# Own copies of the weight units around the joint normalisations, and an order of work that follows expected durations

## The chip, the cores and the metric

The kernel is one program on one core of a Trainium2 chip. The metric is device time in microseconds (us), lower is better. The engines are TensorE (PE), VectorE (DVE), ScalarE (ACT), GpSimd (POOL) and SyncE (SP), which issues the large loads. Each runs its own instructions in the order in which the program gives them to it, and they meet only at semaphores.

## The reference

Two transformer blocks of two layers each, in float32, on 256 tokens of width 1024. The first has one stream, x. The second has two: x (stream A here) and a context (stream B), and both go through the same weights:

```
x = first_block(x)                       # A alone ("solo")
for l in 0, 1:                           # second block
    x     = half_step(x);  ctx = half_step(ctx)        # norm, SwiGLU ffn
    q,k,v = norm(x) @ w_in;  same for ctx              # in2 (layer 1: k, v only for ctx)
    x     = x + attention(...) @ w_out                 # att2, out2; for ctx in layer 0 only
    x     = half_step(x)                               # for ctx in layer 0 only
```

`norm` is x * rsqrt(mean(x*x) + eps) * gain + shift. An attention is softmax(q k) v with a bias, a window or a sink.

## The kernel before

A weight matrix is cut into 510 units of 128 x 1024 floats (512 KB). SP loads a unit into a ring of RAW = 6 buffers. Every product is made of three matmuls on a high and a low part of each operand, so each unit is split before use: ACT writes the high part (`act.activation(... ACT.Copy)`, L1291) into a ring of HIGH = 4 buffers, then DVE writes the low part over the raw one (L1617). A split of unit g waits on ACT for two things: the load of g, and the matmuls of the last stream that uses unit g - 4. DVE's half waits for ACT's.

A *visit* is one stream's step in its stage: either the 24 matmuls of one unit, or (where the step has no unit) a piece of other work on PE, ACT, DVE and POOL. `ORDER` is one list of all 1030 visits, and all engines walk through it. In block 1 only A has visits. In the joint stages (the second block up to B's last one) the list alternates: A opens a unit, B uses it two units later (LAG = 2), and the unit's buffers are free after B's visit. `v.final` marks the visit after which a unit is free. Before each final visit of a unit g, ACT and DVE are given the split of unit g + 3 (AHEAD), which waits for the user of unit g - 1. SP gets the load of g + 6 after it.

A norm is four visits. norm0: DVE adds the last result to X (`finish_update`), ACT squares X, PE sums the squares (L895, 32 matmuls with one column). norm1: DVE forms the variance (L1652), POOL takes the power (L734), DVE corrects it (L1654 to L1656), PE spreads it over the partitions (L882). norm2 and norm3: DVE scales (L1704), ACT writes the high part (L1332), DVE the low part (L1713), for eight tiles of X. The first matmul of the next stage waits for the first of these tiles.

In the joint ffn of the second block each final visit also carries one unit of the modulation parameters (`v.ada`), which is two passes of DVE (L1629).

An attention group is three visits: 3i (PE transposes of the probabilities of group i, which DVE has scaled, L1834), 3i + 1 (PE's weighted sum, L980), 3i + 2 (scores of group i + 2, L962, with DVE's bias L1812 or window L1807 and its maximum, L1815 or L1817). A has 16 groups over 512 keys, B 16 over 256.

The list around one of the joint borders (from ffn to in2, layer 0), with f for the last use of a unit:

```
A65  B63f(split after B62)  Anorm0  B64f(split after B63)  Anorm1  B65f(split after B64)
Anorm2  Bnorm0  Anorm3  Bnorm1  A0  Bnorm2  A1  Bnorm3  A2  B0f(split after B65) ...
```

There are five such norms for each stream: entering the second block (here called border 0), ffn to in2 (1), out2 to ffn (2), ffn to the ffn of layer 1 (3), and ffn to in2 of layer 1 (4).

Of the kernel before, what the change touches and what calls it, by code (L numbers as in the profile page):

```python
# [28 lines left out]
RAW = 6  # L29
HIGH = 4  # L30
AHEAD = 3
LAG = 2
# [48 lines left out]
class Block:  # L81


    def __init__(self, kind, n_units, u, l=0, blk=0, m0=0, pairs=0, ffn=0):
        self.kind, self.n_units, self.u = kind, n_units, u
        self.l, self.blk, self.m0, self.pairs, self.ffn = l, blk, m0, pairs, ffn
# [30 lines left out]
PLAN, TOTAL = make_plan()  # L117
# [140 lines left out]
STAGES, COUNT = make_streams()  # L258


class Visit:


    def __init__(self, s, stage, i, unit):
        self.s, self.stage, self.i, self.unit = s, stage, i, unit
        self.g, self.final, self.ada = None, False, 0


def make_order():

    todo = {s: [Visit(s, st, i, u) for st in STAGES[s] for i, u in enumerate(st.steps)] for s in "AB"}
    joint = next(i for i, v in enumerate(todo["A"]) if not v.stage.solo)
    shared = {v.unit for v in todo["B"] if v.unit is not None}
    order = todo["A"][:joint]
    a, b = todo["A"][joint:], todo["B"]
    open_units = []
    ia = ib = 0

    def b_may():

        if ib >= len(b):
            return False
        u = b[ib].unit
        if u is None:
            return True
        if u not in open_units:
            return False
        ahead = len(open_units) - open_units.index(u) - 1
        return ahead >= LAG or ia >= len(a) or a[ia].unit is None or a[ia].unit not in shared

    def a_may():
        return ia < len(a) and (a[ia].unit is None or len(open_units) <= (LAG if a[ia].unit in shared else 0)) \
            and not (a[ia].stage.solo and ib < len(b)) \
            and not (a[ia].stage.kind == "att2" and ib < len(b) and b[ib].stage.kind == "in2")

    while ia < len(a) or ib < len(b):
        moved = False
        if a_may():
            if a[ia].unit in shared:
                open_units.append(a[ia].unit)  # L300
            order.append(a[ia])
            ia += 1
            moved = True
        if b_may():
            if b[ib].unit is not None:
                open_units.remove(b[ib].unit)
            order.append(b[ib])
            ib += 1
            moved = True
        assert moved, (ia, ib)  # L310
    units = []
    at = {}
    for v in order:
        if v.unit is None:
            continue
        if v.unit not in at:
            at[v.unit] = len(units)
            units.append(v.unit)
        v.g = at[v.unit]
        v.final = v.s == "B" or v.unit not in shared  # L320
    assert sorted(units) == list(range(TOTAL["u"]))
    return order, units


ORDER, UNITS = make_order()


def place_ada():

    t = 0  # L330
    for v in ORDER:
        st = v.stage
        if v.unit is None or not v.final or t >= ADA_UNITS:
            continue
        if st.kind == "ffn" and st.blk == 1:
            n, half = v.i % 36 if v.i < 36 else v.i - 36, 24 if v.i < 36 else 20
            if n >= half and (n - half) % 2 == 1 and t < 3 * KT:
                v.ada = 1
        elif st.kind == "ffn" and st.blk == 2:
            v.ada = 1  # L340
        t += v.ada
        if st.blk == 1 and st.kind == "ffn" and st.l == DEPTH - 1 and v.i == len(st.steps) - 1:
            v.ada += max(0, 3 * KT - t)
            t = max(t, 3 * KT)
    assert t == ADA_UNITS, t


place_ada()


# [147 lines left out]
def build_kernel(nc, xT, ctxT, wstream, adastream, par, const, imask, cond, outT):  # L498
    with ExitStack() as ctx:
# [182 lines left out]
        @block.sync  # L682
        def _(sp):
            half = KT // 2
            sp.dma_start(A.X[:, 0:half, :], xT[:, 0:half, :]).then_inc(S.x_in, 16)
            sp.dma_start(A.X[:, half:KT, :], xT[:, half:KT, :]).then_inc(S.x_in, 16)
            sp.dma_start(CON[:, :], const).then_inc(S.con_in, 16)
            sp.dma_start(PAR[:, :], par).then_inc(S.par_in, 16)

            def load(g):  # L690

                if g >= RAW:
                    s, n = FREED[g - RAW]
# [12 lines left out]
            sp.dma_start(MASKI[:, :], imask).then_inc(S.mask_in, 16)  # L706
            sp.dma_start(SC[:, :, :], cond).then_inc(S.cond_in, 16)
            sp.dma_start(B.X[:, :, :], ctxT).then_inc(S.ctx_in, 16)
            for t in range(ADA_RING):
                load_ada(t)  # L710
            t = ADA_RING
            for v in ORDER:
                for _ in range(v.ada):
                    if t < ADA_UNITS:
                        load_ada(t)
                        t += 1
                if v.final and v.g + RAW < TOTAL["u"]:
                    load(v.g + RAW)
            st = STAGES["A"][-1]
            sp.wait_ge(A.sem.evac, st.old.tok)  # L720
            sp.dma_start(outT[:, 0:half, :], A.X[:, 0:half, :]).then_inc(S.stored, 16)
            sp.wait_ge(A.sem.upd, st.upd + 1)
            sp.dma_start(outT[:, half:half + 2, :], A.X[:, half:half + 2, :]).then_inc(S.stored, 16)
            sp.wait_ge(A.sem.evac, st.old.tok + 1)
            sp.dma_start(outT[:, half + 2:KT, :], A.X[:, half + 2:KT, :]).then_inc(S.stored, 16)
            sp.wait_ge(S.stored, 48)
# [554 lines left out]
        @block.scalar  # L1281
        def _(act):
            def split(g):

                if g >= TOTAL["u"]:
                    return
                act.wait_ge(S.raw_in[g % RAW], 16 * (g // RAW + 1))
                if g >= HIGH:
                    s, n = FREED[g - HIGH]
                    act.wait_ge(streams[s].sem.done, n)  # L1290
                act.activation(W_hi[:, g % HIGH, :], W_raw[:, g % RAW, :], ACT.Copy).then_inc(S.w_hi, 1)  # L1291
# [293 lines left out]
            for g in range(AHEAD):  # L1585
                split(g)
            at_step = {}
            conditioned = False
            for v in ORDER:
                if v.final:  # L1590
                    split(v.g + AHEAD)
                if v.i == 0:
                    at_step[v.s] = table[v.stage.kind](streams[v.s], v.stage)
                next(at_step[v.s])
                if not conditioned and v.stage.kind == "mix1":
                    act.wait_ge(S.cond_in, 16)
                    act.activation(SC[:, :, :], SC[:, :, :], ACT.Silu).then_inc(S.cond_ready, 1)
                    conditioned = True
# [3 lines left out]
        def _(dve):  # L1602
# [7 lines left out]
                dve.wait_ge(S.dve_step, count.steps)  # L1610

            def split(g):

                if g >= TOTAL["u"]:
                    return
                dve.wait_ge(S.w_hi, g + 1)
                dve.tensor_tensor(W_lo[:, g % RAW, :], W_raw[:, g % RAW, :], W_hi[:, g % HIGH, :].bitcast(F32),  # L1617
                                  ALU.subtract).then_inc(S.w_lo, 1)
# [562 lines left out]
            for g in range(AHEAD):  # L2181
                split(g)
            at_step = {}
            for v in ORDER:
                if v.final:
                    split(v.g + AHEAD)
                if v.i == 0:
                    at_step[v.s] = table[v.stage.kind](streams[v.s], v.stage)
                next(at_step[v.s])
                for _ in range(v.ada):  # L2190
                    ada()
# [149 lines left out]
```

## Time and profile before

| | before |
|---|---|
| median of 3 runs | 2898.03 us (2895.4 to 2902.16) |
| profiled execution | 2903.61 us, span 2901.7 us |
| PE busy | 89% of the span |
| DVE / ACT busy | 56% / 34% |
| mean granted TensorE clock | 0.912 of full |
| loads of weight units | 510, 512 KB each |

A busy share says how long an engine had an instruction in it. A PE at half clock is as busy as one at full clock, so the granted clock is read beside it.

### The profile page before, as it was taken

Reading aid. Unit: us, or ns where it says so; the run is one execution under the profiler, and the core shown is the slowest. Engines: PE = TensorE matmul, PEld = TensorE weight load, DVE = VectorE, ACT = ScalarE, POOL = GpSimd, SP = SyncE. Lnnn points to the kernel's source line nnn. Section 1 sums busy time; section 2 is a strip of 40 time slices with the busy share of each in tenths; the row PEclk is TensorE's granted clock in tenths of the full one; section 3 lists DMA queues with packets and bytes.
Section 4 is the critical chain, followed back from the end, with each engine's and each line's share of the span. In section 5 each row is a group of like instructions: output and inputs, shape, how many; then the busy total and the mean of one; then the engine's idle time right before and its main releaser. Section 6 shows DMA issues by size and latency. Waiting matters only on the chain.

```text
span 2901.7 us, 48201 instructions
## 1 busy us (share of the span) xinstructions
PE 2596.7 (89%) x20772; PEld 2527.4 (87%) x20772; DVE 1627.3 (56%) x2686; ACT 988.2 (34%) x1441; POOL 180.6 (6%) x300
## 2 busy tenths in 40 slices
PE   7789998799799999887658999999999999766999
PEld 7679987799799999887548999999999999645999
DVE  5558877478677777524453777754333333433554
ACT  5345544365332222311442322223222222133443
POOL 0000000170000000011000710000000001000000
PEclk9779988699799999898789999998999999777999
DMA  6225643156435555311001455531222222100454
GB/s 222 72 89 193 225 174 106 59 187 233 160 130 182 189 185 187 108 53 59 1 1 50 130 190 187 185 132 66 94 95 95 95 88 74 59 0 21 147 188 155
DMA packets 104020, 352.82 MB, mean 122 GB/s; under 512 B 18816, under 2 KB 18944, under 8 KB 103424
## 3 DMA queue, kind: packets, MB, share of 16 engines
q1 hardware_dynamic: 95616, 348.94, 35.3%
q8 instruction: 164, 2.69, 0.4%
q0 software_dynamic: 8192, 0.80, 0.3%
q14 instruction: 48, 0.39, 0.0%
HBM read 348.63 MB, written 1.05 MB: 121 GB/s over the span
## 4 chain that ended last, share of the span: by engine, by line
PE 58%; issue 7%; DVE 4%; ACT 2%; POOL 1%; POOLq 0%; DVEq 0%; ACTq 0%
PE slot L833 17%; PE slot L834 17%; PE slot L835 17%; PE slot L895 1%; PE slot L980 1%; PE slot L971 1%; PE slot L873 1%; POOL R0B L734 1%; ACT PTSA L1390 1%; PE slot L962 1%; PE slot L861 1%; PE slot L884 1%; PE slot L864 0%; PE slot L863 0%; DVE PRA L1834 0%
## 5 line engine op out<-in xcount | busy, mean ns | idle before, releaser
L1617 DVE TENSOR_TENSOR W_lo<-W_raw,W_hi 128x1024 fp32r<-128x1024 f32 x510 | 623.5, 1224 | 768.4 <-ACT W_hi L1291 763.6
L1291 ACT ACTIVATE W_hi<-W_raw 128x1024 fp32r<-128x1024 f32 x510 | 538.9, 1059 | 1251.4 <-PE slot L835 1113.2
L833 PE MATMUL slot<-H_hiA,W_lo 128*128 128x256 f32 x2864 | 820.4, 286 | 21.9 <-DVE VA L2040 6.5
L834 PE MATMUL slot<-H_loA,W_hi 128*128 128x256 f32 x2864 | 813.7, 284 | 0.0
L835 PE MATMUL slot<-H_hiA,W_hi 128*128 128x256 f32 x2864 | 812.3, 284 | 0.0
L833 PEld LDWEIGHTS slot<-H_hiA,W_lo 128*128 128x128 f32 x2864 | 551.8, 193 | 30.5 <-issue 15.9
L834 PEld LDWEIGHTS slot<-H_loA,W_hi 128*128 128x128 f32 x2864 | 552.4, 193 | 0.0
L835 PEld LDWEIGHTS slot<-H_hiA,W_hi 128*128 128x128 f32 x2864 | 551.4, 193 | 0.0
L833 PE MATMUL slot<-H_hiB,W_lo 128*128 128x256 f32 x1280 | 361.0, 282 | 4.4 <-DVE VB L2040 4.4
L834 PE MATMUL slot<-H_loB,W_hi 128*128 128x256 f32 x1280 | 360.5, 282 | 0.0
L835 PE MATMUL slot<-H_hiB,W_hi 128*128 128x256 f32 x1280 | 359.6, 281 | 0.0
L1629 DVE SCALAR_TENSOR_TENSOR PROD<-A_raw,SC 128x1024 bf16<-128x1024 f32 x288 | 340.7, 1220 | 6.7 <-DVEq L1663 5.1
L833 PE MATMUL slot<-HIDA,W_lo 128*128 128x256 f32 x1056 | 295.2, 280 | 0.8 <-DVE HIDA L1795 0.8
L834 PE MATMUL slot<-HIDA,W_hi 128*128 128x256 f32 x1056 | 295.2, 280 | 0.0
L835 PE MATMUL slot<-HIDA,W_hi 128*128 128x256 f32 x1056 | 294.8, 279 | 0.0
L833 PEld LDWEIGHTS slot<-H_hiB,W_lo 128*128 128x128 f32 x1280 | 243.3, 190 | 5.0 <-DVE VB L2040 4.8
L834 PEld LDWEIGHTS slot<-H_loB,W_hi 128*128 128x128 f32 x1280 | 242.7, 190 | 0.0
L835 PEld LDWEIGHTS slot<-H_hiB,W_hi 128*128 128x128 f32 x1280 | 242.6, 190 | 0.0
L833 PEld LDWEIGHTS slot<-HIDA,W_lo 128*128 128x128 f32 x1056 | 198.3, 188 | 1.2 <-issue 1.2
L835 PEld LDWEIGHTS slot<-HIDA,W_hi 128*128 128x128 f32 x1056 | 198.0, 187 | 0.0
L834 PEld LDWEIGHTS slot<-HIDA,W_hi 128*128 128x128 f32 x1056 | 198.0, 187 | 0.0
L734 POOL TENSOR_TENSOR R0A<-V_A,EXPO 128x2 f32<-128x2 f32 (+3 forms) x25 | 35.1, 1402 | 2320.8 <-DVE V_A L1652 2320.8
(258 smaller groups left out, 3391.8 us busy)
## 6 DMA issues: line engine op xcount, KB each, us to landing
W_raw<-wstream SPq DMA_DIRECT2D x510, 512.0 KB, 3.6
A_raw<-adastream SPq DMA_DIRECT2D x144, 512.0 KB, 3.5
BT<-par POOLq DMA_DIRECT2D x256, 3.0 KB, 2.7
CON<-const SPq DMA_DIRECT2D x1, 1025.5 KB, 7.9
XA<-xT SPq DMA_DIRECT2D x2, 512.0 KB, 4.6
SC<-cond SPq DMA_DIRECT2D x1, 1024.0 KB, 14.8
XB<-ctxT SPq DMA_DIRECT2D x1, 1024.0 KB, 16.5
PAR<-par SPq DMA_DIRECT2D x1, 684.0 KB, 9.1
```

Of the source, the lines that this page charges most:

```text
L734: pool.tensor_tensor(s.R0[:, 0:n], s.V_[:, 0:n], EXPO[:, 0:n], ALU.pow).then_inc(s.sem.r0, 1)
L833: pe.matmul(out, wl, xh, start=start, stop=False, skip_group_check=True)
L834: pe.matmul(out, wh, xl, start=False, stop=False, skip_group_check=True)
L835: return pe.matmul(out, wh, xh, start=False, stop=stop, skip_group_check=True)
L861: pe.matmul(out, s.H_lo[:, kt, tk], wh[:, c], start=q == 0 and k == 0, stop=False, skip_group_check=True)
L873: mm = pe.matmul(p[:, 0, width * c:width * c + width], b, rhs, start=c == 0 and i == 0, stop=i == len(tiles) - 1, skip_group_check=True)
L884: mm = pe.matmul(out[64 * h:64 * h + 64], src[:, h:h + 1].to_broadcast([P, 64]), ident, start=True, stop=True, skip_group_check=True)
L895: mm = pe.matmul(p[:, 0, tt:tt + 1], s.SQ[kt // 4][:, kt % 4, P * tt:P * tt + P], con("ones", 1), start=kt == 0 and tt == 0, stop=kt == KT ...
L962: mm = pe.matmul(p[:, h, SEQ * n:SEQ * n + SEQ], g.q[b], k[b], start=True, stop=True, skip_group_check=True)
L1291: act.activation(W_hi[:, g % HIGH, :], W_raw[:, g % RAW, :], ACT.Copy).then_inc(S.w_hi, 1)
L1617: dve.tensor_tensor(W_lo[:, g % RAW, :], W_raw[:, g % RAW, :], W_hi[:, g % HIGH, :].bitcast(F32), ALU.subtract).then_inc(S.w_lo, 1)
L1629: a = dve.scalar_tensor_tensor(PROD[:, b, :], A_raw[:, slot, :], 1.0, SC[:, b, :], ALU.mult, ALU.mult, accum_out=MOD[:, t // MODS, t % MOD ...
```

## The change

Four things in the list of visits; no arithmetic changes.

1. Around the joint norms the last four units of a stage and the first four of the next are no longer shared: A and B each load and split a copy (`edge_units`, EDGE = 4). There are 32 more units, 542 in place of 510.
2. The joint part of the list is built by expected durations (`expected`, `start`): at each point the stream whose next visit can start first by these numbers goes first, A on a tie. A visit of a stream's own unit needs all shared units to be closed. A may open a shared unit only when B's next unit is a shared one.
3. A split is put in the list as soon as it can be: before the first visit, of any kind, that comes after the last user of unit g - 4. Before, it stood at the next final visit of a unit. This holds in the solo stages too.
4. The modulation units are carried by shared units' last visits only.

The list around the same border after the change:

```
A61(split after B58)  B59f  B60f(split after B59)  B61f(split after B60)
A62f  A63f  A64f  A65f(each: split after the visit before)  B62f(split after A65)
Anorm0(split after B62)  B63f  B64f(split after B63)  Anorm1(split after B64)  Anorm2  Anorm3  B65f
A0f(split after B65)  A1f  A2f  A3f  Bnorm0(split after A3)  Bnorm1  Bnorm2  Bnorm3  B0f  B1f  B2f  B3f  A4 ...
```

At border 0 it is Anorm0 Bnorm0 Anorm1 Anorm2 Anorm3 Bnorm1 A0 A1 A2 A3 Bnorm2(split after A3) Bnorm3 B0. At border 4, where only A has the first units of in2, it is A0 to A4, Bnorm0, A5, A6, Bnorm1, A7, A8, Bnorm2, Bnorm3, B0. The joint attention had A and B in turns; now it is A(3i+2) A(3i+3) B(3i+2) B(3i+3) A(3i+4) B(3i+4). In solo stages the split moves from the next unit's visit to a step without a unit in front of it, five norms (norm0 or final0) among them.

```diff
+EDGE = 4
+def edge_units():
+    out = set()
+    for st in STAGES["A"]:
+        if st.solo:
+            continue
+        if st.kind == "ffn":
+            out |= set(st.steps[:EDGE]) | set(st.steps[-EDGE:])
+        if st.kind == "in2":
+            out |= set(st.steps[:4])
+        if st.kind == "out2":
+            out |= set(st.steps[-EDGE:])
+    return out
+
+def expected(v):
+    st, i = v.stage, v.i
+    if v.unit is not None:
+        first = i == 0 and st.kind in ("ffn", "in2", "mix1")
+        return 2.75, [(3, 3.0)] if first else [(1, 0.8)] if i == 0 else []
+    if st.kind in ("norm", "final"):
+        return ((3.6, [(1, 2.6)]), (0.5, [(1, 3.3)]), (0.0, []), (0.0, []))[min(i, 3)]
...
+    if st.kind == "att2":
+        c = 1.2 if v.s == "A" else 0.7
+        if i < 2:
+            return c, []
+        k = (i - 2) // 3
+        if (i - 2) % 3 == 0:
+            return c, [(i - (k if k < 2 else 3 * k - 2), 5.5)]
+        return c, [(1, 1.4)]
+    return 0.0, []
...
-    while ia < len(a) or ib < len(b):
...
+        if not v.shared:
+            return not open_units
+        if s == "B":
+            return v.unit in open_units
+        ahead = next((b for b in todo["B"][at["B"]:] if b.unit is not None), None)
+        return len(open_units) <= LAG and ahead is not None and ahead.shared
...
+    while any(at[s] < len(todo[s]) for s in "AB"):
+        can = [s for s in "AB" if may(s)]
+        s = min(can, key=start)
+        v = todo[s][at[s]]
+        now = start(s) + expected(v)[0]
...
+    for v in order:
+        while n_split < len(units) and (n_split < HIGH or n_split - HIGH in used):
+            v.splits.append(n_split)
+            n_split += 1
+        if v.final:
+            used.add(v.g)
+        while n_load < len(units) and n_load - RAW in used:
+            v.loads.append(n_load)
+            n_load += 1
...
-        elif st.kind == "ffn" and st.blk == 2:
+        elif st.kind == "ffn" and st.blk == 2 and v.shared:
             v.ada = 1
...
             for v in ORDER:
-                if v.final:
-                    split(v.g + AHEAD)
+                for g in v.splits:
+                    split(g)
                 if v.i == 0:
                     at_step[v.s] = table[v.stage.kind](streams[v.s], v.stage)
                 next(at_step[v.s])
```

## Rows read from the trace of the kernel before

**Rows 1.** The page: busy time by engine, and shares of the chain.
```profile
PE   2596.7 (89%) x20772; PEld 2527.4 (87%) x20772; DVE 1627.3 (56%) x2686; ACT 988.2 (34%) x1441; POOL 180.6 (6%) x300
...
PE 58%; issue 7%; DVE 4%; ACT 2%; POOL 1%; POOLq 0%; DVEq 0%; ACTq 0%
```

**Rows 2.** Stretches: length, busy time by engine, granted clock, DMA share, GB/s.
```profile
600.00:700.00 100.00, 100.00 (x851) 100.00 (x850) 82.68 (x122) 54.74 (x71) 36.75 (x78) 1.00 0.66 220
...
1178.00:1211.00 33.00, 25.46 (x143) 25.20 (x142) 21.93 (x53) 12.04 (x21) 1.39 (x2) 0.64 0.28 96
1585.50:1613.60 28.10, 21.29 (x131) 21.03 (x130) 15.80 (x40) 9.47 (x16) 4.00 (x3) 0.70 0.17 57
1979.70:2009.70 30.00, 24.84 (x141) 24.59 (x140) 16.39 (x42) 10.86 (x19) 1.41 (x2) 0.66 0.16 53
2374.50:2402.10 27.60, 22.35 (x136) 22.09 (x135) 16.12 (x39) 10.93 (x18) 1.39 (x2) 0.69 0.17 58
```

**Rows 3.** The chain that ended last, in order of time: start, us, what.
```profile
1189.88 2.37 DVE PROD L1629 x4
1192.25 0.41 DVE TMPA L1704
...
1196.51 6.97 PE slot L895 x32
1203.75 0.71 POOL R0B L734
1205.08 0.69 PE slot L882 x2
...
1585.51 3.46 PE slot L895 x32
...
1610.25 0.69 PE slot L882 x2
...
2004.20 0.69 PE slot L882 x2
...
2397.73 0.69 PE slot L882 x2
```

**Rows 4.** ACT and DVE, instructions in order of time, around border 1.
```profile
1173.43 1.04 ACT L1314 ACTIVATE SQA<-XA 128x1024 f32<-128x1024 f32 x1
...
1187.64 1.06 ACT L1291 ACTIVATE W_hi<-W_raw 128x1024 fp32r<-128x1024 f32 x1 [7.39 <-PE slot L835]
...
1188.73 1.23 DVE L1617 TENSOR_TENSOR W_lo<-W_raw,W_hi 128x1024 fp32r<-128x1024 f32 x1 [3.50 <-ACT W_hi L1291]
...
1195.98 1.65 DVE L1674 SCALAR_TENSOR_TENSOR XB<-slot,GATE,XB 128x256 f32<-128x256 f32 x4
...
1197.67 0.63 ACT L1320 ACTIVATE SQB<-XB 128x512 f32<-128x512 f32 x1 [0.15 <-DVE XB L1674]
...
1203.51 0.16 DVE L1652 TENSOR_SCALAR V_B<-slot 128x2 f32<-128x2 f32 x1 [2.05 <-PE slot L895]
...
1206.95 0.48 DVE L1713 SCALAR_TENSOR_TENSOR H_loB<-TMPB,MOD,H_hiB 128x256 fp32r<-128x256 f32 x1 [0.18 <-ACT H_hiB L1332]
```

**Rows 5.** One cycle of the joint attention, in order of time.
```profile
1396.62 0.71 PE L962 MATMUL slot<-KA,QA 64*128 64x256 f32 x4 [0.26 <-DVE H_loA L1845]
...
1400.01 0.68 DVE L1815 TENSOR_REDUCE NMB<-slot 128x2 f32<-128x512 f32 x1
...
1401.74 1.68 PE L971 MATMUL slot<-CON,PRA 128*128 128x128 f32 x8 [3.54 <-DVE PRA L1834]
1401.79 0.62 DVE L1834 TENSOR_SCALAR PRB<-PRB,RIB 128x256 f32<-128x256 f32 x2
...
1403.21 1.06 PE L971 MATMUL slot<-CON,PRB 128*128 128x128 f32 x4
1403.46 1.02 ACT L1390 ACTIVATE PTSA<-slot 128x1024 f32<-128x1024 f32 x1 [0.97 <-PE slot L971]
...
1407.24 0.71 PE L962 MATMUL slot<-KA,QA 64*128 64x256 f32 x4 [0.26 <-DVE H_loA L1845]
```

More of the change, by code:

```diff
@@ L265, in __init__ @@
         self.s, self.stage, self.i, self.unit = s, stage, i, unit
-        self.g, self.final, self.ada = None, False, 0
+        self.g, self.shared, self.final, self.ada = None, False, False, 0
+        self.splits, self.loads = [], []
+EDGE = 4
[18 more added lines that the diff above has]
+        return ((3.6, [(1, 2.6)]), (0.5, [(1, 3.3)]), (0.0, []), (0.0, []))[min(i, 3)]
+    if st.kind == "in2":
+        after = i > 0 and st.steps[i - 1] is None
+        sums = sum(u is None for u in st.steps[:i]) % 2 == 0
+        return (1.9, [(1, 0.5)]) if sums else (3.6, [(1 if after else 2, 2.8)])
+    if st.kind == "att2":
[7 more added lines that the diff above has]
+    return 0.0, []
 def make_order():
@@ L272, in make_order @@
     joint = next(i for i, v in enumerate(todo["A"]) if not v.stage.solo)
-    shared = {v.unit for v in todo["B"] if v.unit is not None}
+    edges = edge_units()
+    shared = ({v.unit for v in todo["A"]} & {v.unit for v in todo["B"]}) - edges - {None}
+    for s in "AB":
+        for v in todo[s]:
+            v.shared = v.unit in shared
     order = todo["A"][:joint]
-    a, b = todo["A"][joint:], todo["B"]
+    todo["A"] = todo["A"][joint:]
+    at = dict(A=0, B=0)
+    end = dict(A=[], B=[])
@@ L276, in make_order @@
     open_units = []
-    ia = ib = 0
-    def b_may():
-        if ib >= len(b):
-            return False
-        u = b[ib].unit
-        if u is None:
-            return True
[L286 to L294, printed above, removed]
@@ L296, in make_order, with may @@
-    while ia < len(a) or ib < len(b):
[L297 to L310, printed above, removed]
+    now = 0.0
+    def may(s):
+        if at[s] >= len(todo[s]):
+            return False
+        v = todo[s][at[s]]
+        other = "B" if s == "A" else "A"
+        if s == "A":
+            behind = next((b for b in todo["B"][at["B"]:]), None)
+            if v.stage.solo and behind is not None:
+                return False
+            if v.stage.kind == "att2" and behind is not None and behind.stage.kind == "in2":
+                return False
+        if v.unit is None:
+            return True
+        if not v.shared:
[4 more added lines that the diff above has]
+        return len(open_units) <= LAG and ahead is not None and ahead.shared
@@ new lines, in start @@
+    def start(s):
+        i = at[s]
+        t = now
+        for back, delay in expected(todo[s][i])[1]:
+            if i >= back:
+                t = max(t, end[s][i - back] + delay)
+        return t
+    while any(at[s] < len(todo[s]) for s in "AB"):
+        can = [s for s in "AB" if may(s)]
+        s = min(can, key=start)
+        v = todo[s][at[s]]
+        now = start(s) + expected(v)[0]
+        end[s].append(now)
+        if v.shared:
+            (open_units.append if s == "A" else open_units.remove)(v.unit)
+        order.append(v)
+        at[s] += 1
@@ L311, in make_order @@
     units = []
-    at = {}
+    opened = {}
     for v in order:
@@ L315, in make_order @@
             continue
[L316 to L321, printed above, removed]
+        v.final = v.s == "B" or not v.shared
+        if v.unit in opened and v.shared:
+            v.g = opened[v.unit]
+            continue
+        opened[v.unit] = v.g = len(units)
+        units.append(v.unit)
+    assert set(units) == set(range(TOTAL["u"]))
+    used = set()
+    n_split, n_load = AHEAD, RAW
+    for v in order:
[7 more added lines that the diff above has]
+            n_load += 1
+        assert v.g is None or v.g < n_split
     return order, units
@@ L716, in _ @@
                         t += 1
-                if v.final and v.g + RAW < TOTAL["u"]:
-                    load(v.g + RAW)
+                for g in v.loads:
+                    load(g)
             st = STAGES["A"][-1]
@@ L1283, in split @@
             def split(g):
-                if g >= TOTAL["u"]:
-                    return
                 act.wait_ge(S.raw_in[g % RAW], 16 * (g // RAW + 1))
@@ L1612, in split @@
             def split(g):
-                if g >= TOTAL["u"]:
-                    return
                 dve.wait_ge(S.w_hi, g + 1)
@@ L2184, in _ @@
             for v in ORDER:
-                if v.final:
-                    split(v.g + AHEAD)
+                for g in v.splits:
+                    split(g)
                 if v.i == 0:
```

## The prediction

> **What bounds the kernel now.** I read the shares of busy time and of the chain first. PE is busy 89% of the span and holds 58% of the chain, with no other engine above 4% [rows 1]. So time can come only from the stretches in which PE stands still or runs at half clock. Then I read stretches. In steady work PE is full, the clock is whole, and 851 matmuls take 100 us, so a visit of 24 matmuls takes 2.82 us; the loads of a solo stage move 220 GB/s beside that [rows 2]. Then I read the four joint borders 1 to 4, each from the start of A's sums to the moment when the clock is whole again: 33.0, 28.1, 30.0 and 27.6 us at a mean granted clock of 0.64 to 0.70 [rows 2].
>
> What would full speed need there? Sums 3.46 us, for A and for B; two visits of B, 5.64; two spreads of 0.35; and the part of A's first visits done by then. A's first visit began 0.69 us after the start of B's spread, so 5.2, 2.7, 4.8 and 3.7 us before the end of the stretch, at half clock, which is 2.6, 1.3, 2.4 and 1.8 us of work [rows 2, 3]. Work is 15.9, 14.6, 15.7 and 15.1 us, and **the loss is 17.1, 13.5, 14.3 and 12.5 us, 57.4 in all**. That is what the change goes for. It is made of B's norm starting late, since DVE has modulation passes and A's scales ahead of it [rows 3, 4]; of the gap around the power; and of half clock: the same 32 sums take 3.46 us at full and 6.97 at half [rows 3].
>
> **Borders 1 to 3 after the change.** A's own four visits are followed by B62, and B63, B64 and B65 are laid between A's norm steps. That order would hide A's norm if ACT and DVE did the norm when its data is there. They don't, because of where the splits now stand. The split at Anorm0 waits for B62, and ACT's squares and DVE's update are behind it. The split at Anorm1 waits for B64, and DVE's variance is behind it. The split at Bnorm0 waits for A3, and B's squares and update are behind it. On PE each of these norm steps comes directly after just that visit. Durations: the high part takes 1.06 us and ends 1.09 after the visit it waits for, the low part is done at 2.3, the squares take 1.04 + 0.63 + 0.63, the update 1.65 [rows 4].
>
> A, from the end of B62 (0): ACT has split at 1.1 and the first squares at 2.1; DVE has split at 2.3 and updated at 4.0; the last squares are there at 4.65. PE stands from 0 to 2.1. The sums then take between 3.6 us (full clock) and 7.0 (half). I take 6.1, since in the rows the clock went down during sums without any gap ahead of them and here there is one, so they end at 8.2. The clock is then low until 4.1 us into full work (the mean of 5.2, 2.7, 4.8 and 3.7). B63 and B64 (5.64 us of work) end at 15.9. Then the split of Anorm1: 1.1 + 1.2, and V, power and correction 1.55 (1203.51 to the spread at 1205.08), together 3.86 us of standing PE. Spread at 19.8, 0.7 us; B65 and A0 to A3, 14.1 us of work with 4.1 us at half clock, end at 36.6. Work in it: 3.46 + 5.64 + 0.35 + 14.1 = 23.55. **Loss 13.1.**
>
> B, from the end of A3 (0): the same 2.1 us and sums to 8.2, then 1.6 to the spread (no split here), and 2.35 from the spread to the first low tile (1205.08 to 1206.95 + 0.48) [rows 3, 4]. B0 starts at 12.15. It is fed one tile in 0.79 us and runs at half clock for 4.1 us, so it ends at 17.1 in place of 3.46 + 0.35 + 2.82 = 6.6. **Loss 10.5.** Nothing covers this chain: A has used up its own four visits, and may open no shared unit before B has done its four.
>
> So 23.6 us a border against 17.1, 13.5 and 14.3: **+25.9**. If the clock never went down it would be 6.1 + 7.2 = 13.3, or -5 in all; if every step runs at half, some 27, or +36. I take the sum nearer the upper end, as the clock went down in all four borders of before.
>
> **Border 4.** A's part is the same 13.1. B's sums come after A4, whose 2.8 us cover the split, but DVE still copies A's first product (1.15) ahead of B's update, so PE stands some 2.7 us before the sums, which with half clock I put at 7 (2.5 to 10.5). 20.1 against 12.5: **+7.6**.
>
> **Border 0.** Before, the scales of A and B come in halves, and A0 starts 0.7 us after the spreads. After, B's correction stands behind all eight scales of A (6.5 us), and PE's A0 is behind B's spread: +7. Then B's scales wait for the split after A3, 2.3 + 1.5 us of standing PE, and the clock goes down again, 2: **+11** (7 to 13).
>
> **Attention of layer 0.** A cycle takes 10.62 us from scores to scores [rows 5]. After, PE has A's transposes, B's scores, B's transposes, A's weighted sum. DVE takes B's maximum only after A's scale, which helps A by 0.65 us. But B's scores now wait for A's transposes, and A's weighted sum waits for B's transposes, in which everything of B is in a row: scores 0.55, maximum 0.68, scale 0.82, transposes 0.9, together some 3.0 us where ACT's copy of A (1.02) was the only step [rows 5]. Net 3.0 - 1.07 - 0.65 = 1.3 us in each of 15 cycles: **+20**. Bounds: 12, if PE overlaps the two sets of transposes as it does now, and 27, since the groups with sinks have two more small steps.
>
> **Solo stages.** In five norms the first squares now wait for the last unit's visit plus a split: PE stands 2.1 us in each where it went on at once: **+10.5** (5 to 12). In mix1 the split comes ahead of the statistics of the gated part and of its scale, of which one 2.3 us is bare in each layer: **+4** (0 to 12). In2 loses one stall (DVE stood in B's power and held A's next unit) and gets another (a copy behind a split that waits for the visit before): **-1** (-8 to +8).
>
> **What costs nothing.** 32 more units are 32 x 1.23 us of DVE, 32 x 1.06 of ACT and 16.8 MB. In the own visits a unit is needed each 2.82 us, which is 186 GB/s, below the 220 moved in the solo stretch with a full PE [rows 2]; DVE and ACT have 0.5 and 1.8 us to spare in each, as the modulation passes are elsewhere. Without that cover, one late split of 2.3 us in four own visits would be +37. The 32 matmul visits themselves exist before as well.
>
> **The sum**: 25.9 + 7.6 + 11 + 20 + 10.5 + 4 - 1 = +78 us. The profiled execution took 2903.6; the median of the runs is 5.6 lower, so 2898 + 78 = **2976**.
>
> All this rests on ACT and DVE doing their queues strictly in order. The rows show it: PE ended the visit ahead of A's spread at 1187.64, yet DVE's first scale came at 1192.25, behind a low part and 2.37 us of modulation passes [rows 3, 4]. The Trainium skill says the same (PSUM — Partial Sum Buffer, section "Engine vs sequencer instructions": the queues of ScalarE, VectorE and GpSimdE are strict FIFO); by that rule the sum is as above, and without it the first rival's. The case's trace agrees, with those 2.4 us.
>
> **Rivals.**
> 1. *The splits hold nothing up (faster)*. ACT and DVE reach the norm in time, so A's norm is hidden. Each border then loses only B's chain, 8.5 us against a mean of 14.4, -24 in all, and in the attention only the 0.65 us in 15 cycles is left, -10: 2864. It decides at one point: whether the squares of A start before B62's end plus 1 us. For it: the first squares of before started at 1173.43, well ahead of the sums [rows 4]. Against: no split stood ahead of them there. Chance 0.09.
> 2. *The clock stays up*. The gaps are there but cost no half clock: borders -5 and +2, border 0 +8, the rest as it is: 2898 + 5 + 20 + 10 + 3 = 2936. For it: own visits are dense. Against: 0.64 to 0.70 in all four stretches [rows 2]. Chance 0.12.
> 3. *Gains and losses cancel* (the borders gain as in 1, attention and solo norms lose): within 0.2% of before. Chance 0.04.
> 4. *More than forecast*: late splits as priced above, or attention at its upper bound, 3010 and above. Chance 0.05.
>
> **How the numbers follow.** The forecast has 0.70. 0.2% is about what a measurement of this kernel can tell from no change (5.8 us). Faster is rival 1 with 0.01 more for gains that I don't see, 0.10; same is rival 3 with 0.01 more, 0.05; slower is the rest, 0.85. The range leaves out rival 1 and most of 3 and 4. Its low end takes rival 2 with the lower bounds of attention and mix1, 2926; its high end takes the forecast with borders at +36 and attention at 27 and late splits in part, 3010.
>
> **What would show it.** In the changed kernel, at each of borders 1 to 4: ACT's first squares of A start about 1.1 us after the end of B62; PE stands some 2 us ahead of A's sums, some 3.9 ahead of A's spread, and twice again around B's norm, with the clock at 0.5. In the joint attention a cycle of 11.9 us. In a solo norm the first squares after a high part. A cycle below 10.6, or a border whose A part has no standing PE, would make the forecast wrong.

## The result and the profile after

| | before | after |
|---|---|---|
| median | 2900.10 us (2895.40 to 2904.45, 4 runs) | 3037.53 us (3035.41 to 3039.31, 4 runs) |
| profiled execution | 2903.61 us, span 2901.7 | 3035.41 us, span 3033.5 |
| mean granted clock | 0.912 | 0.894 |
| PE busy | 2596.7 us (89%) | 2628.1 us (87%) |

The change makes the kernel slower: ratio 1.0474, 95% interval 1.0455 to 1.0493. That is +137 us in the medians and +132 in the two profiled spans. The direction is that of the forecast (+78); the time lies 27 us above its range.

The page of after, against [rows 1]: busy time by engine, then the shares of the chain by engine.

```profile
PE 2628.1 (87%) x20772; PEld 2544.4 (84%) x20772; DVE 1668.9 (55%) x2718; ACT 1025.1 (34%) x1473; POOL 180.6 (6%) x300
...
PE 58%; issue 7%; DVE 4%; POOL 3%; ACT 1%; POOLq 0%; DVEq 0%; ACTq 0%
```

PE issues the same 20772 matmuls and is busy 31 us longer, and the mean granted clock is lower, so more of them ran at half clock; and POOL has gone from 1% to 3% of the chain with the same 180.6 us of work. Those two points of the chain, some 60 us, hold the term that the forecast hadn't.

**Border 1** went as it was forecast. The steps on ACT, DVE and PE in after (start us, us, engine, line; in brackets the idle time before and who ended it), against [rows 4]; L1359 and L1682 are the two halves of a split, L1382 the first squares, L966 the sums, L1717 the variance, L953 the spread:

```profile
1193.03 1.06 ACT L1359 ACTIVATE W_hi<-W_raw 128x1024 fp32r<-128x1024 f32 x1 [0.67 <-PE slot L906]
1193.99 1.04 ACT L1382 ACTIVATE SQA<-XA 128x1024 f32<-128x1024 f32 x1
...
1194.12 1.23 DVE L1682 TENSOR_TENSOR W_lo<-W_raw,W_hi 128x1024 fp32r<-128x1024 f32 x1 [0.50 <-ACT W_hi L1359]
...
1195.18 5.66 PE L966 MATMUL slot<-CON,SQA 128*128 128x1 f32 x32 [2.25 <-ACT SQA L1382]
...
1210.54 1.23 DVE L1682 TENSOR_TENSOR W_lo<-W_raw,W_hi 128x1024 fp32r<-128x1024 f32 x1 [1.96 <-ACT W_hi L1359]
1211.68 0.15 DVE L1717 TENSOR_SCALAR V_A<-slot 128x2 f32<-128x2 f32 x1
...
1213.26 0.43 PE L953 MATMUL slot<-CON,RSA 128*128 128x128 f32 x2 [3.90 <-DVE RSA L1721]
...
1229.45 1.06 ACT L1359 ACTIVATE W_hi<-W_raw 128x1024 fp32r<-128x1024 f32 x1 [1.77 <-PE slot L906]
1230.41 1.04 ACT L1382 ACTIVATE SQB<-XB 128x1024 f32<-128x1024 f32 x1
...
1231.60 4.63 PE L966 MATMUL slot<-CON,SQB 128*128 128x1 f32 x32 [2.24 <-ACT SQB L1382]
```

PE stands 2.25 us ahead of A's sums, 3.90 ahead of A's spread and 2.24 ahead of B's sums, each time behind a split that waited for the visit just before. Half clock behind each, in windows (length, busy time and count of PE, PEld, DVE, ACT, POOL, granted clock, DMA share, GB/s):

```profile
1196.00:1206.00 10.00, 10.00 (x51) 10.00 (x52) 0.92 (x3) 1.26 (x2) 0.00 (x0) 0.53 0.01 4
1213.00:1218.00 5.00, 4.75 (x27) 4.75 (x28) 4.18 (x12) 2.43 (x5) 0.00 (x0) 0.66 0.00 0
1234.00:1245.00 11.00, 7.58 (x36) 6.97 (x36) 6.64 (x19) 3.90 (x8) 0.70 (x1) 0.53 0.00 1
```

From such windows, one microsecond each, I made a loss for every part of the kernel: PE's standing time, plus its busy time multiplied by (1 - granted clock). Rows that read "busy 10.00, clock 0.53" lose 4.7 us.

**Border 2** did not go as forecast. The last entries of POOL's queue there, in order of time (L805 is the power, L809 clears the bias table BT, L817 is its 128 small DMAs), and the window in which they run:

```profile
1656.81 2.66 POOL L809 MEMSET BT<- 128x3072 f32 x1
1662.86 60.95 POOL L817 DMA_DIRECT2D BT<-par  x128 [3.39 <-issue]
1723.82 0.72 POOL L805 TENSOR_TENSOR R0B<-V_B,EXPO 128x2 f32<-128x2 f32 x1
```
```profile
1670.00:1725.00 55.00, 8.62 (x63) 8.35 (x61) 4.86 (x11) 4.32 (x5) 54.53 (x115) 0.57 0.13 31
```

POOL is busy for 54.53 of 55 us while PE is busy for 8.62. DVE had formed B's variance at 1680.90:

```profile
1680.90 0.16 DVE L1717 TENSOR_SCALAR V_B<-slot 128x2 f32<-128x2 f32 x1 [3.36 <-PE slot L966]
```

The chain of after says who held whom (start us, us, what):

```profile
1663.40 60.40 POOL BT L817 x127
...
1723.82 0.73 POOL R0B L805
...
1725.18 0.70 PE slot L953 x2
```

B's power (0.73 us) sits in POOL's queue behind the table for the attention of layer 1. In the kernel before, the same queue had the other order:

```profile
1608.91 0.69 POOL L734 TENSOR_TENSOR R0B<-V_B,EXPO 128x2 f32<-128x2 f32 x1 [18.96 <-DVE V_B L1652]
1609.56 2.66 POOL L738 MEMSET BT<- 128x3072 f32 x1
1615.61 60.97 POOL L746 DMA_DIRECT2D BT<-par  x128 [3.39 <-issue]
```

The table is issued at the first visit of A's ffn. With its own copies A reaches that visit before B's norm1, where before it came behind it. This is the strict order of GpSimdE's queue that the Trainium skill names (PSUM — Partial Sum Buffer, section "Engine vs sequencer instructions"); the trace agrees, with 42.9 us between the start of B's variance and that of its power, which needs nothing else.

**The attention of layer 0.** One cycle of after, scores to scores, against [rows 5] (L1033 scores, L1880 maximum, L1899 scale, L1042 transposes, L1051 weighted sum, L1458 ACT's copy):

```profile
1459.51 0.71 PE L1033 MATMUL slot<-KA,QA 64*128 64x256 f32 x4
...
1464.03 1.97 PE L1042 MATMUL slot<-CON,PRA 128*128 128x128 f32 x8 [3.37 <-DVE PRA L1899]
1465.92 1.23 PE L1033 MATMUL slot<-KB,QB 64*128 64x256 f32 x4
1466.03 1.02 ACT L1458 ACTIVATE PTSA<-slot 128x1024 f32<-128x1024 f32 x1 [1.56 <-PE slot L1042]
1467.20 0.69 DVE L1880 TENSOR_REDUCE NMB<-slot 128x2 f32<-128x512 f32 x1 [3.23 <-PE slot L1033]
...
1468.00 0.62 DVE L1899 TENSOR_SCALAR PRB<-PRB,RIB 128x256 f32<-128x256 f32 x2
...
1468.67 1.11 PE L1042 MATMUL slot<-CON,PRB 128*128 128x128 f32 x4 [1.52 <-DVE PRB L1899]
1469.71 1.12 PE L1051 MATMUL slot<-PTSA,VA 128*64 128x128 f32 x4
...
1473.29 0.71 PE L1033 MATMUL slot<-KA,QA 64*128 64x256 f32 x4
```

B's scores, maximum, scale and transposes do stand in a row between A's transposes and A's weighted sum, but the cycle is 13.8 us, not 11.9. The whole stretch, before and then after:

```profile
1371.00:1544.00 173.00, 106.37 (x755) 88.83 (x753) 84.37 (x207) 76.06 (x222) 0.00 (x0) 0.81 0.00 1
```
```profile
1395.00:1602.00 207.00, 124.86 (x753) 95.65 (x752) 84.56 (x206) 79.11 (x222) 0.00 (x0) 0.69 0.00 1
```

It is 34 us longer. PE stands 15.5 us more (82.1 against 66.6), and the same matmuls keep it busy 18.5 us longer, at a clock of 0.69 in place of 0.81. My forecast had the first of these only.

**The ledger.** Predicted, and measured as the difference of the losses of the two profiles:

| part | predicted | measured |
|---|---|---|
| solo norms, mix1, in2 | +13.5 | +14.3 |
| border 0 | +11 | +10.3 |
| borders 1 and 3 | +15.8 | +14.7 |
| border 2, without the table | +10.1 | +9.8 (loss in e1_pool_late) |
| border 2, B's power behind the table | 0 | +40.2 (63.7 against 23.5 in e1_pool_late) |
| border 4 | +7.6 | +7.2 |
| attention of layer 0 | +20 | +32.1 |
| sum | +78 | +128.6 (the spans differ by 131.8) |

Border 0 begins behind the spread of block 1's final norm (at 784 us in before, 792 in after), and border 4 reaches to B's spread (2397.73 and 2543.62). The medians differ by 137.4 us, 5.6 more than the spans, since the profiled execution of before took 3.5 us more than its median and that of after 2.1 less.

### The profile page after: what moved, and what is told of

It reads as the page before. It is cut to its first block, busy times and chain, and to the rows that moved or that the text cites. A ratio compares the mean times of both kernels' runs of the same rounds, so it can differ in the third digit from the quotient of the medians.

```text
span 3033.5 us, 48329 instructions
## 1 busy us (share of the span) xinstructions
PE 2628.1 (87%) x20772; PEld 2544.4 (84%) x20772; DVE 1668.9 (55%) x2718; ACT 1025.1 (34%) x1473; POOL 180.6 (6%) x300
## 4 chain that ended last, share of the span: by engine, by line
PE 58%; issue 7%; DVE 4%; POOL 3%; ACT 1%; POOLq 0%; DVEq 0%; ACTq 0%
PE slot L904 17%; PE slot L905 16%; PE slot L906 16%; POOL BT L817 2%; PE slot L1051 1%; PE slot L1042 1%; PE slot L966 1%; PE slot L1033 1%; PE slot L944 1%; ACT W_hi L1359 1%; PE slot L955 1%; PE slot L932 1%; PE slot L934 1%; PE slot L935 0%; DVE PRA L1899 0%
## 5 line engine op out<-in xcount | busy, mean ns | idle before, releaser
L1682 DVE TENSOR_TENSOR W_lo<-W_raw,W_hi 128x1024 fp32r<-128x1024 f32 x542 | 663.5, 1225 | 829.1 <-ACT W_hi L1359 824.2
L1359 ACT ACTIVATE W_hi<-W_raw 128x1024 fp32r<-128x1024 f32 x542 | 573.6, 1059 | 1370.8 <-PE slot L906 1200.0
L904 PE MATMUL slot<-H_hiA,W_lo 128*128 128x256 f32 x2864 | 816.8, 285 | 20.1 <-DVE VA L2105 7.2
L904 PE MATMUL slot<-H_hiB,W_lo 128*128 128x256 f32 x1280 | 367.4, 287 | 14.6 <-DVE H_loB L1778 9.4
L1694 DVE SCALAR_TENSOR_TENSOR PROD<-A_raw,SC 128x1024 bf16<-128x1024 f32 x288 | 340.9, 1221 | 12.8 <-DVEq L1728 10.8
L805 POOL TENSOR_TENSOR R0A<-V_A,EXPO 128x2 f32<-128x2 f32 (+3 forms) x25 | 35.0, 1401 | 2483.6 <-DVE V_A L1717 2483.6
```

What stands on the lines that cost most here:

```text
L805: pool.tensor_tensor(s.R0[:, 0:n], s.V_[:, 0:n], EXPO[:, 0:n], ALU.pow).then_inc(s.sem.r0, 1)
L904: pe.matmul(out, wl, xh, start=start, stop=False, skip_group_check=True)
L1694: a = dve.scalar_tensor_tensor(PROD[:, b, :], A_raw[:, slot, :], 1.0, SC[:, b, :], ALU.mult, ALU.mult, accum_out=MOD[:, t // MODS, t % MOD ...
```

## The experiments

Ten further kernels ran, two of them twice, each with runs of the kernel before beside it. Ratios are to those. The loss at a border is that of the ledger, from the profiled execution. For border 4, the expectation of e12 names 11.9 us of e9, from a window that runs on into a wait of in2; up to B's spread and the half clock behind it the loss is 9.4.

| kernel | ratio, 95% interval | us against before (ratio less 1, times 2900) | losses at borders 1, 2, 3, 4 |
|---|---|---|---|
| before | 1 | | 17.4, 13.7, 14.6, 12.7 |
| after | 1.0474 [1.0455, 1.0493] | +137 | 22.0, 63.7, 24.7, 19.9 |
| e1_pool_late | 1.0338 [1.0310, 1.0366] | +98 | 23.4, 23.5, 21.8, 19.9 |
| e2_att_turns | 1.0324 [1.0277, 1.0371] | +94 | 23.6, 65.8, 24.7, 19.9 |
| e3_split_old | 1.0208 [1.0175, 1.0241] | +60 | 11.4, 56.0, 10.8, 7.9 |
| e4_only_split | 1.0224 [1.0185, 1.0263] | +65 | 28.2, 26.4, 28.5, 26.3 |
| e5_only_att | 1.0182 [1.0149, 1.0214] | +53 | 17.2, 15.5, 12.6, 14.6 |
| e6_clean | 0.9953 [0.9935, 0.9972] | -14 | 8.3, 10.2, 9.8, 7.0 |
| e7_tie | 1.0022 [1.0008, 1.0035] | +6 | 16.9, 14.6, 14.2, 14.0 |
| e8_split_not_norm | 0.9996 [0.9983, 1.0009] | -1 | 17.3, 15.5, 14.5, 12.8 |
| e9_b_later | 0.9920 [0.9893, 0.9946] | -23 | 12.4, 12.3, 8.2, 9.4 |
| e10_shared | 1.0104 [1.0062, 1.0147] | +30 | 24.0, 22.3, 23.2, 16.3 |
| e11_clean_again | 0.9938 [0.9923, 0.9953] | -18 | 9.1, 10.2, 10.8, 8.0 |
| e12_b_later_again | 0.9950 [0.9935, 0.9965] | -15 | 12.2, 10.6, 10.1, 7.8 |

### The three causes, each undone

**e1_pool_late**: the table eight visits of A later; nothing else changes.

```diff
-                if s is A and st.blk == 2 and st.l == 0 and st.ffn == 1:
-                    pool.wait_ge(s.sem.done, st.v)
-                    bias_table(1)
-                for _ in st.steps:
+                for n in range(len(st.steps)):
+                    if n == 8 and s is A and st.blk == 2 and st.l == 0 and st.ffn == 1:
+                        pool.wait_ge(s.sem.done, st.v)
+                        bias_table(1)
                     yield
```

> The changed kernel, with GpSimd's bias table for layer 1 (a fill and 128 small DMAs, some 67 us in the changed kernel's trace, 1656.9 to 1723.8) issued at A's ninth step of that ffn, behind B's norm, in place of A's first, ahead of it. Theory: B's norm of border 2 waits for POOL's power, which stands behind the table, and border 2 costs 50.7 us more than before, of which the forecast's mechanisms explain some 10. Expected 2994 to 3000 us, 40 us below the changed kernel. Rival (the gap of border 2 has another cause, and the table only happens to lie there): within 5 us of 3037.

Measured: 2992.86 us (2981.54 to 2996.94), 39 us less than after by the ratios. The profiled spans differ by 54 us, but the losses by 41.4: the profiled execution is the fastest of the four, and the 12 us between the two figures fit the other rate of matmuls of the last section. POOL's queue in this kernel:

```profile
1672.06 0.70 POOL L805 TENSOR_TENSOR R0B<-V_B,EXPO 128x2 f32<-128x2 f32 x1 [24.29 <-DVE V_B L1717]
1672.70 2.66 POOL L809 MEMSET BT<- 128x3072 f32 x1
1678.76 61.19 POOL L817 DMA_DIRECT2D BT<-par  x128 [3.39 <-issue]
```

The table takes as long as ever, and nobody waits for it. The loss at border 2 falls from 63.7 to 23.5, the size of borders 1 and 3. The queue is shown as the cause, and its price is about 40 us (39 in the medians, 40.2 in the loss).

**e2_att_turns**: the joint attention in turns, as before the change.

```diff
         s = min(can, key=start)
+        if all(t in can and todo[t][at[t]].stage.kind == "att2" for t in "AB"):
+            s = min(can, key=lambda t: todo[t][at[t]].i)
```

> The changed kernel, with A and B in turns again in the joint attention of layer 0, all else as it is. The stretch takes 207 us in the changed kernel and 172 before. Theory: all of it is the order of the visits, so 35 us come back: about 3002 us and a cycle of 10.6 us. By the price in the prediction (1.3 us a cycle) 20 come back: 3017. Rival (the attention is longer for what comes ahead of it, the clock or late data): under 10 come back.

Measured: 2992.98 us (2972.85 to 3001.18), 43 us less than after by the ratios and 34 in the profiled spans. The attention is that of before again, in length, busy time and clock:

```profile
1394.00:1567.00 173.00, 106.61 (x763) 89.56 (x761) 82.47 (x207) 76.69 (x224) 0.00 (x0) 0.81 0.00 1
```

**e3_split_old**: the splits stand again at the final visit of a unit.

```diff
-        while n_split < len(units) and (n_split < HIGH or n_split - HIGH in used):
-            v.splits.append(n_split)
-            n_split += 1
         if v.final:
+            if v.g + AHEAD < len(units):
+                v.splits.append(v.g + AHEAD)
+                n_split = v.g + AHEAD + 1
```

> The changed kernel, with the splits back at the visits that had them before (ahead of each last use of a unit g, the split of g + 3), the own copies and the order kept. Theory of the prediction: at borders 1, 3 and 4 some 10 us each come back (PE no longer stands for a split ahead of A's sums, of A's spread and of B's sums), at border 0 four, in the solo stages 8, at border 2 only A's part, as B's waits for POOL: some 45 in all, 2992 us (2975 to 3005). Rival (the place of a split costs nothing, since the unit's own visit would wait for it as long): within 10 us of 3037.

Measured: 2958.16 us (2946.58 to 2963.30), 77 us less than after. The losses at borders 1, 3 and 4 are half those of after or less (11.4, 10.8, 7.9) and now below those of before; the 56.0 at border 2 is the table, which is still in the way. The joint stretch at border 1 in this kernel, and then the same length in after:

```profile
1172.00:1238.00 66.00, 60.13 (x463) 58.76 (x462) 37.96 (x66) 30.43 (x40) 2.38 (x3) 0.90 0.42 138
```
```profile
1188.00:1254.00 66.00, 54.20 (x377) 53.03 (x377) 34.57 (x62) 26.73 (x36) 1.39 (x2) 0.82 0.35 114
```

### The parts alone, on the kernel before

**e4_only_split**: the loop of e3's diff, with its sign turned, put into the kernel before; shared units and turns stay.

> The kernel before, with the splits' new place alone: shared units and the order of before. Theory: the solo norms and steps lose the 8 us that the changed kernel lost by the start of the second block, and the joint borders and in2 some more, as the split of a unit that was just used stands ahead of norm steps: 2900 + 8 + 5 to 20 = 2913 to 2928 us. Rival (the place costs only with own copies): 2900 to 2908.

Measured: 2963.61 us (2946.96 to 2970.81), +65. The borders lose 26 to 28 us, more than in after. I take it that there is even less to cover a late norm without own units; no run shows that by itself.

**e5_only_att**: the kernel before, with the joint attention listed in pairs. It was meant to have the order of after, and it hasn't.

```diff
+    sizes = [2] + [1, 2] * 16
+    for k in sizes:
+        for s in "AB":
+            new += left[s][:k]
+            del left[s][:k]
```

> The kernel before, with the changed order of the joint attention of layer 0 alone (A3i+2 A3i+3 B3i+2 B3i+3 A3i+4 B3i+4). Theory: the order alone makes the cycle 13.8 us in place of 10.6, half of it by steps of B that stand in a row and half by the clock, which is half during the matmuls of a cycle with gaps: 34 us more, 2933. The prediction's price was 20: 2919. Rival (the slower cycle came with the state in which the changed kernel entered the stretch): under 10 more.

Measured: 2947.20 us (2941.25 to 2953.72), +53. After the two leading scores of each stream this list takes one visit, the transposes, and then two, the weighted sum and the next scores. In after, scores and transposes stand together and the weighted sum alone. PE in e5 (L982 transposes, L991 weighted sum, L973 scores):

```profile
1434.71 1.97 PE L982 MATMUL slot<-CON,PRA 128*128 128x128 f32 x8 [1.78 <-DVE PRA L1845]
...
1437.80 1.11 PE L991 MATMUL slot<-PTSA,VA 128*64 128x128 f32 x4 [0.26 <-ACT PTSA L1401]
...
1440.98 0.71 PE L973 MATMUL slot<-KA,QA 64*128 64x256 f32 x4 [0.69 <-DVE H_loA L1856]
...
1446.48 1.17 PE L973 MATMUL slot<-KB,QB 64*128 64x256 f32 x4 [3.77 <-DVE H_loB L1856]
```

So e5 measures a third order: PE stands 3.77 us ahead of B's scores, for a tile that DVE makes of B's result, a wait that the cycle of after doesn't have. From its first to its last scale of B the attention takes 213 us here, 162 in before and 197 in after. The expectation, which was for the order of after, stays untested. That the order of after costs what the ledger says rests on e2 alone, which puts the order of before back.

**e8_split_not_norm**: e4 with one condition, so that no split is put ahead of a norm step.

```diff
-        while n_split < len(units) and (n_split < HIGH or n_split - HIGH in used):
+        while v.stage.kind not in ("norm", "final") and n_split < len(units) and (n_split < HIGH or n_split - HIGH in used):
```

> The kernel before, with the splits' new place everywhere but at norm steps (norm and final visits take none; the split goes to the next visit). With all splits moved it took 65 us more. Theory: the cost lies at the norms, 14 at each of four joint borders and 8 in the solo stages: 2900 to 2912. Rival (it is spread over in2, mix1 and the ffn): 2940 or more.

Measured: 2897.15 us (2891.43 to 2900.27), no difference from before. The cost of e4 is the splits ahead of norm steps; elsewhere an early split makes no difference that these runs could tell.

### What is left when the three are undone

**e6_clean**: e1, e2 and e3 together; own copies and the order by durations stay.

> The changed kernel with the three suspected costs taken out: the table behind B's norm on GpSimd, the attention in turns, the splits at their old visits. What is left of the change are the own copies and the order by durations outside the attention. Theory: the copies and the order as such are a small gain, 3 to 4 us at each border (from the kernel with the old splits, whose stretch from norm to norm took 391.3 us where before took 394.8): 2880 to 2892. Rival (32 more loads and splits cost something everywhere): 2905 or more.

Measured: 2886.39 us (2871.68 to 2891.93, 10 runs), ratio 0.9953, and again in **e11_clean_again**: 2880.12 us (2879.13 to 2881.66, 4 runs), 0.9938. It beats the kernel before by 14 and 18 us, and so the kernel after by 151 and 155. Undone one at a time, the three causes gave 39, 43 and 77 us back, 159 together: they add up to within 8 us.

> The kernel e6_clean once more, on the same chip as the two above: 2880 to 2892, ratio 0.993 to 0.998 to the kernel before. Profiled border losses of 7 to 10 us again, against 13 to 17 in the kernel before.

Borders 1 to 4 lose 38.1 us in e11 and 58.4 in before. Border 0 loses 6.5 more than in before, and the part behind border 4 loses 7.8 less; why that part gains wasn't tested.

**e10_shared**: e6 without the own copies.

```diff
-    return out
+    return set()
```

> The kernel e6_clean without the four own copies at the borders: both streams share the four units again, and only the order by expected durations is left. If e6's gain on the kernel before comes from the copies (A's own visits stand ready while B's norm runs), this one comes out with the kernel before, 2895 to 2905, with border losses of some 13 us. If it comes from the order of the norm steps alone, it comes out with e6, 2882 to 2892, with border losses of 7 to 10 us.

Measured: 2935.75 us (2913.72 to 2937.92), ratio 1.0104, so +30, and 56 above e11_clean_again. Neither expectation held: the order by durations without copies is worse than before. PE around border 1, in e10_shared and then in e11_clean_again (L955 spread, L968 sums):

```profile
1203.57 6.96 PE L968 MATMUL slot<-CON,SQB 128*128 128x1 f32 x32 [7.62 <-ACT SQB L1384]
```
```profile
1181.35 3.70 PE L968 MATMUL slot<-CON,SQA 128*128 128x1 f32 x32 [0.78 <-ACT SQA L1384]
1193.43 0.43 PE L955 MATMUL slot<-CON,RSA 128*128 128x128 f32 x2 [1.08 <-DVE RSA L1723]
```

With shared units B's norm is listed right behind A's, and PE stands 7.62 us until ACT and DVE are through A's scales. With copies four visits of A lie between. So e6 needs the copies for its gain, and the order by durations without them loses 30. The copies under the order of before were not run, so what they are worth by themselves is not shown.

**e7_tie**: e6, but on a tie the step without a unit goes first, so that B's norm0 comes after A0 and its norm1 after A2.

```diff
-        s = min(can, key=start)
+        s = min(can, key=lambda t: (start(t), todo[t][at[t]].unit is not None))
```

> As the one before, and on a tie of expected starts the step without a unit goes first, so that B's norm0 comes after A0 and its norm1 after A2, with A's own visits between. Theory: B's norm at borders 1 to 3 was bare because A had used up its four own visits, which the prediction put at 10.5 us a border with the split and some 8 without; laid between them it is hidden but for the half clock: 15 to 25 us below the kernel before this one, 2860 to 2875. Rival (the bare time is set by DVE's and ACT's work, which is the same): within 5 us of the kernel before this one.

Measured: 2903.56 us (2897.84 to 2906.76), ratio 1.0022: a miss. ACT and DVE in e7_tie ahead of B's squares and around B's update, then PE's sums (L1402 and L1780 make A's input tiles, L1361 and L1684 split, L1384 are the squares, L1741 updates):

```profile
1198.50 0.51 ACT L1402 ACTIVATE H_hiA<-TMPA,MOD 128x256 fp32r<-128x256 f32 x1 [0.28 <-DVE TMPA L1771]
1198.92 1.99 ACT L1361 ACTIVATE W_hi<-W_raw 128x1024 fp32r<-128x1024 f32 x2
1200.81 1.04 ACT L1384 ACTIVATE SQB<-XB 128x1024 f32<-128x1024 f32 x1
...
1198.64 0.89 DVE L1780 SCALAR_TENSOR_TENSOR H_loA<-TMPA,MOD,H_hiA 128x256 fp32r<-128x256 f32 x2 [0.17 <-DVEq L1730]
1199.99 2.36 DVE L1684 TENSOR_TENSOR W_lo<-W_raw,W_hi 128x1024 fp32r<-128x1024 f32 x2 [0.46 <-ACT W_hi L1361]
1202.27 1.65 DVE L1741 SCALAR_TENSOR_TENSOR XB<-slot,GATE,XB 128x256 f32<-128x256 f32 x4
...
1201.99 4.34 PE L968 MATMUL slot<-CON,SQB 128*128 128x1 f32 x22 [3.40 <-ACT SQB L1384]
```

PE, which had used up A0, stood for 3.4 us from 1198.6, and what it waited for was ACT: A's tiles and two splits last until 1200.9 there, and B's first squares come behind them. DVE is held up in the same way, by A's tiles until 1199.5 and splits until 1202.3, and B's update, which the later squares need, comes only then.

**e9_b_later** is e7 with B's norm0 behind A1 and its norm1 behind A2, and **e12_b_later_again** repeats it.

```diff
-        return ((3.6, [(1, 2.6)]), (0.5, [(1, 3.3)]), (0.0, []), (0.0, []))[min(i, 3)]
+        w0, w1 = (2.6, 3.3) if v.s == "A" else (5.4, 2.7)
+        return ((3.6, [(1, w0)]), (0.5, [(1, w1)]), (0.0, []), (0.0, []))[min(i, 3)]
```

> The kernel e7_tie with B's norm steps given longer expected delays, so that at a joint border PE's list reads A0, A1, B's first norm step, A2, B's sums of variance, the rest of B's norm, A3, B0. In e7 PE stood 3.4 us ahead of B's sums since the update of B on VectorE stands behind A's scales. If that wait is the cost of e7, one more visit of A ahead (2.8 us) covers most of it at each of four borders and the time lies below e7 by 8 to 12 us, 2888 to 2895, or with the half clock gone as well at 2865 to 2885. Rival: at a border B's norm then stands wherever VectorE lets it, the wait moves to A3 or B0 (B's scales follow later by as much as its sums), and the time is e7's, 2900 to 2907.

> The kernel e9_b_later once more, with more rounds, to tell whether it is below the kernel e6_clean or level with it. If the extra visit of A ahead of B's sums is worth something, the ratio to the kernel before is again at 0.990 to 0.993 and its interval ends below 0.9953, the middle of e6_clean's first ten runs. If the first result (ratio 0.992 over four runs) was the luck of faster stretches of matmuls, it comes out at 0.994 to 0.997. The border losses of the profile (12.4, 12.3, 8.2 and 11.9 us at borders 1 to 4, against 9.1, 10.2, 10.8 and 8.0 in e11_clean_again) speak for the second.

Measured: 2872.36 us (2869.77 to 2885.27, 4 runs), ratio 0.9920, then 2883.28 us (2872.61 to 2887.85, 12 runs), 0.9950. Below e7 by 20 us or more both times; against e6 and e11 (0.9953 and 0.9938) the first was ahead and the second, with three times the runs, level. That the two orders differ is not shown.

## Why the prediction was right and wrong

**Right: what the splits do at a norm.** The claim was that a norm step now waits for the visit just before it. The trace has the squares 1.0 us behind the end of the visit, PE standing 2.25, 3.90 and 2.24 us where I had 2.1, 3.9 and 2.1, and half clock behind each. Borders 1, 3 and 4 lose 22.0, 24.7 and 19.9 us, forecast 23.6, 23.6 and 20.1; border 0 loses 10.3 more than before, forecast 11. e3 (-77 us when undone) and e8 (e4 without splits at norm steps is level with before) show the mechanism by itself. At border 1 the A part lost 12.8 us (forecast 13.1) and the B part 9.2 (10.5): the rows of before gave these to within a microsecond or so, as the durations of a split, of the squares and of the update don't change.

**Right: the 32 more loads and splits.** In the ffn stretches between the borders the loss is 0.0 us in both kernels.

**Wrong: POOL's queue, 40 us.** The failed step is a wait: in the border part, B's "1.6 to the spread (no split here)", used for borders 1 to 3 alike. At border 2 it took 44.3 us from B's variance (1680.90) to B's spread (1725.18). I moved A0 to A3 ahead of B's norm1 and followed what they carry on PE, ACT, DVE and SP, but not what the first visit of a stage carries on POOL. The trace of before has it: a clear of 2.66 us and then 61 us of small DMAs, begun 0.65 us after the start of B's power. It would have been the dearest line of the sum.

**Wrong in size: the attention, +20 for +32.** The mechanism (B's four steps in a row with A's) is in the rows, and e2 gives it back. The term that was too small is the work in the cycle: I took durations of PE from a cycle at clock 0.84. Longer pauses bring more half clock: PE's busy time in a cycle went from 6.56 to 8.91 us, its standing from 4.06 to 4.89. I had priced half clock at the borders, from rows, and not here.

**Right in sum by luck: the solo parts.** Solo norms, mix1 and in2 lost 14.3 us more, forecast 13.5, but not where the forecast had it. The norms of block 1 with its final norm lost some 16 more, above the range of 5 to 12 that I gave for all five; the two mix1 stages lost 7 less, where I had 4 more; the part behind border 4 lost 6.5 more. The norms' share is of the splits: with e3 the loss up to the final norm is 139.0 (140.1 in before, 146.8 in after) and behind border 4 128.3 (134.7 and 141.2).

**The rivals.** *The splits hold nothing up* needed A's squares ahead of the end of B62 plus 1 us; they came 1.0 us behind it, after the 0.96 us that ACT took for the split. *The clock stays up* fell with the rows at 0.53. *More than forecast* had the wrong mechanism: no late splits in own visits, and the attention above its upper bound of 27. The chance of 0.05 for it was too low: my sum had seven terms, each with its bounds, and none of the bounds was for a queue that I hadn't followed. With the table out of the way (e1) the time is 2993 us, inside the range of 2926 to 3010; without the 40.2 us the miss would have been the attention alone.

## What to carry to other kernels

When a planner may reorder visits, list what each moved visit issues on every engine, the rare things too (a table, a broadcast, a clear that only the first visit of a stage carries), and look at what now stands behind each of them in that queue; here a 61 us job was harmless behind B's power and cost 40 us ahead of it. "As early as possible" is not free for work that waits: put on an in-order queue ahead of work whose data is there, it delays that work by its own wait. And where a change lengthens pauses of PE in work that is already at mixed clock, price the matmuls of that stretch at half clock too.

## What the hardware showed that I had not expected

At a granted clock of 1.00, with PE full, matmuls of one form run at two rates. In e1_pool_late, earlier and later in the same execution:

```profile
850.00:950.00 100.00, 100.00 (x885) 100.00 (x884) 73.18 (x106) 27.46 (x36) 0.00 (x0) 1.00 0.52 181
...
2200.00:2300.00 100.00, 100.00 (x851) 100.00 (x850) 31.93 (x40) 22.12 (x24) 0.00 (x0) 1.00 0.28 95
```

That is 113.0 ns a matmul against 117.5. The kernels before and after were at 851 or 852 per 100 us wherever I looked. The other rate isn't tied to the loads (181 GB/s here; 183 GB/s in before at the other rate), and nothing in the trace says what sets it. Among the profiled executions, e5_only_att has the other rate too, again at 850 to 1150 us; both are the fastest of their kernel's runs. Where it lasts it changes the span by some 4% of the stretch, here about 12 us. That it makes the runs of one kernel spread by up to 1% is a guess, not shown. Verdicts here go by medians and their intervals for that reason.
